# The last roots of an attention block as logarithm and exponential, and an output slab that starts on the finished tiles

## The chip, the cores and the metric

The kernel runs on one core of a Trainium2 chip. The metric is device time in microseconds (us) of one execution; shown is the median of the runs of a kernel. The engines are TensorE (PE, with its weight loads PEld), VectorE (DVE), ScalarE (ACT), GpSimd (POOL) and the DMA queue of SyncE (SP). Each engine works through its own instructions in order and waits on semaphores for the others.

## The reference, cut to what matters

One block of a model with three mixers side by side (a linear recurrent unit "LRU", an attention with forget gates "fox", and a recurrent mixer "rwkv"), whose outputs are joined and multiplied by one output matrix; a mixture of experts and two more layers follow.

```python
def rms_norm(x, g, eps=1e-6):
    return x * lax.rsqrt(jnp.mean(x * x, axis=-1, keepdims=True) + eps) * g

ya = rms_norm(gelu(gate_in) * h, lru_norm_g)                # 256 wide
o  = softmax(mask(q k^T * scale + c_i - c_j)) v             # 8 heads of 64, 512 tokens
yb = rms_norm(o, fox_norm_g)                                # 512 wide
yc = ((o_r - mean) * lax.rsqrt(var + 64e-5) * ln_g + ln_b + bonus) * g   # 256 wide
y  = concatenate([ya, yb, yc], axis=-1)
x  = x + y @ w_out
x  = x + hier_moe(rms_norm(x, norm2_g), ...)
```

## The kernel before, in words

Tokens (512) lie along the free dimension, features in tiles of 128 partitions, so a 1024-wide activation is eight tiles of 128x512. Matmul inputs are split in two parts: a tile is cast to fp32r (`y_hi`), the rest is kept (`y_lo = y - y_hi`), and three products (hi·hi, lo·hi, hi·lo) are summed. Weights come as slabs of 128x2048: SP loads `raw`, ACT casts `w_hi` (L218), POOL subtracts `w_lo` (L227).

The change lies in two blocks of code and in the step between them. The first block ends with the attention's loop over 32 units (`UNITS`: eight heads for the query block of tokens 384 to 511, then for 256 to 383, 128 to 255 and 0 to 127, so keys shrink from 512 to 128). No scheduler orders it: each engine has its own loop over n, and what stands at `if n == 24` is the order. In turn n:

- PE computes the scores of unit n into one of two banks (L1115, L1117), turns the probabilities of unit n-2 (L1127) and weighs the values of unit n-3 (L1137). The scores of n wait until the exponential of n-2 has read their bank; the weighing waits for ACT's copy of the turned probabilities.
- DVE takes the row maximum of unit n (L1739), later the inverse of the row sum (L1750), and from unit 16 on scales the weighed output into the token-major tile `o_tok` (L1729).
- ACT takes the exponential of unit n (L1427) and copies the turned probabilities of n-2 (L1401); up to unit 15 it scales the outputs (L1408). After the last head of a query block it squares that block with a sum (L1412).

The rest of the three mixers is spread over the turns. LRU's and rwkv's row sums are copied out (L1774, n = 17), their roots taken by ACT with those of the first two attention blocks at n = 21 (L1417, L1458, L1459), inverted by DVE at n = 22 (L1717, L1778), spread by PE over the partitions with matmuls against the identity (LRU at n = 24, L1088; rwkv at 25 and 26, L1098) and multiplied in by DVE (LRU L1784 at n = 24; rwkv L1705 and L1706 at 25 and 26). The first two attention blocks are turned at 27 and 28 (L1144) and written to `Y` at 28 and 29 (L1723). After the loop blocks three and four follow together: ACT loads the table of the square root (L1435), squares the last block, takes two roots; DVE inverts and scales; PE turns eight pieces (L1144); DVE writes `Y`.

Then the stage closes: an end of block on every engine, semaphores cleared, a barrier of all engines. The second block begins with ACT casting the eight tiles of `Y` to `y_hi` (L1941), DVE subtracting (L1946), and PE working through the first output slab tile by tile (L277 to L279, each tile 6 matmuls), each tile waiting for its `y_lo`. Three more slabs follow without a pause on PE; DVE adds each to `xT` (L1959), which SP loads anew at the start of this block.

A function of ACT needs its table in the engine; the built program holds an ACT_TABLE_LOAD wherever the next function is not in the table that is loaded.

Of the kernel before, what the change touches and what calls it, by code (L numbers as in the profile page):

```python
# [22 lines left out]
F32 = mybir.dt.float32  # L23
# [6 lines left out]
P = 128  # L30
# [117 lines left out]
def build(nc, t):  # L148
    with ExitStack() as whole:
# [486 lines left out]
        o_tok, o_sq = [M[:, n] for n in (0, 1, 8, 9)], T[:, 2]  # L636
# [81 lines left out]
        sums_out, lru_spread, ln_spread = (stage_sem(n) for n in ("sums_out", "lru_spread", "ln_spread"))  # L718
        gate_row = [stage_sem(f"gate_row{n}") for n in range(4)]
# [78 lines left out]
        def _(pe):  # L798
# [285 lines left out]
            def spread_lru():  # L1084
                pe.wait_ge(sums_out, 2)
# [61 lines left out]
            for n in range(len(UNITS) + 3):  # L1147
# [26 lines left out]
                if n in (27, 28):  # L1174
                    pe.wait_ge(y_rwkv, n - 26)
                    turn_block(n - 27, (seq_wu, seq_so)[n - 27])
            pe.wait_ge(y_fox, 2)
            pe.wait_ge(sc_exp, len(UNITS))
            for i in range(2, TB):
                turn_block(i, pd[i - 2])  # L1180

        @block.scalar
        def _(act):
# [231 lines left out]
            def block_roots(i, count):  # L1415
                act.wait_ge(fox_sq, i + count)
                act.activation(small[:, 48 + i:48 + i + count], small[:, 44 + i:44 + i + count], ACT.Sqrt, bias=EPS,  # L1417
                               scale=1.0 / 512).then_inc(fox_root, 1)

            for n in range(len(UNITS) + 4):  # L1420
# [13 lines left out]
                if n == len(UNITS) + 1:  # L1434
                    act.preload_act_table(ACT.Sqrt)  # L1435
# [15 lines left out]
                if n in (12, 14):  # L1451
                    j = (n - 12) // 2
                    act.wait_ge(lru_val, j + 1)
                    act.activation(lru_sqr[:, j], lh[:, j], ACT.Square).then_inc(lru_sq, 1)
                if n == 21:
                    block_roots(0, 2)
                    act.wait_ge(sums_out, 1)
                    act.activation(small[:, 64:68], small[:, 64:68], ACT.Sqrt, bias=EPS, scale=1.0 / 256)  # L1458
                    act.activation(small[:, 68:84], small[:, 68:84], ACT.Sqrt, bias=GN_EPS,  # L1459
                                   scale=1.0 / CH).then_inc(ln_root, 1)  # L1460
                if n == 26:
                    act.wait_ge(y_lru, 2)
                    split_next(act, IN1_PAIRS - 1, 1)
            block_roots(2, 2)

        @block.vector
        def _(dve):
# [264 lines left out]
            for n in range(len(UNITS) + 4):  # L1732
# [53 lines left out]
                if n in (25, 26):  # L1786
                    rwkv_out(n - 25)
                if n in (28, 29):
                    block_out(n - 28, (seq_wu, seq_so)[n - 28])
            block_inverses(2, 2)  # L1790
            for i in range(2, TB):
                scale_block(i)
            for i in range(2, TB):
                block_out(i, pd[i - 2])
# [6 lines left out]
        y_hi = sb("y_hi", [P, KT, TOK], F32R)  # L1801
        y_lo = sb("y_lo", [P, KT, TOK], F32R)
        V, QK, MG = (sb(n, [P, KT, TOK]) for n in ("V", "QK", "MG"))
# [52 lines left out]

        stage2_loaded = sem("stage2_loaded")
# [66 lines left out]
        def y_vector(dve, v, m, j, value, n, yb, vb, tj=None, wait=None):  # L1924
# [12 lines left out]
            dve.wait_ge(y_ready, yb + 2 * n + 2)  # L1937

# [153 lines left out]
        def _(pe):  # L2092
# [351 lines left out]
        def _(act):  # L2444
            a = steps["scalar"].again(act)
            round_scalar(act, Y, 0)
# [14 lines left out]
            for n in range(4):  # L2461
# [898 lines left out]
```

## Time and profile before

| | us |
|---|---|
| median of 3 runs | 2642.66 (2641.64 to 2643.73) |
| the profiled execution, its own time | 2649.67 |
| its span, first to last instruction | 2647.9 |
| PE busy | 2592.0 (98%) |
| ACT busy | 1109.7 (42%) |
| DVE busy | 1545.8 (58%) |
| mean granted clock of PE | 0.987 |

A row of the timeline gives the start in us, how long the group was busy, the engine, the line of the kernel, the operation, output<-inputs, shapes, how many instructions were merged, and in square brackets how long the engine stood idle before it and whose work released it. "Granted clock" is a share of full speed: 1.00 is 2.4 GHz, 0.50 is 1.2 GHz.

### The profile page before, as it was taken

Reading aid. Unit: us, or ns where it says so; the run is one execution under the profiler, and the core shown is the slowest. Engines: PE = TensorE matmul, PEld = TensorE weight load, DVE = VectorE, ACT = ScalarE, POOL = GpSimd, SP = SyncE. Lnnn points to the kernel's source line nnn. Section 1 sums busy time; section 2 is a strip of 40 time slices with the busy share of each in tenths; the row PEclk is TensorE's granted clock in tenths of the full one; section 3 lists DMA queues with packets and bytes.
Section 4 is the critical chain, followed back from the end, with each engine's and each line's share of the span. In section 5 each row is a group of like instructions: output and inputs, shape, how many; then the busy total and the mean of one; then the engine's idle time right before and its main releaser. Section 6 shows DMA issues by size and latency. Waiting matters only on the chain.

```text
span 2647.9 us, 32566 instructions
## 1 busy us (share of the span) xinstructions
PE 2592.0 (98%) x12974; PEld 2138.6 (81%) x12974; DVE 1545.8 (58%) x1718; ACT 1109.7 (42%) x1309; POOL 876.4 (33%) x203
## 2 busy tenths in 40 slices
PE   7999889999999999999999999999999999999998
PEld 5777778888788888888888888888888888888887
DVE  5584545999775383364674346855563463835445
ACT  5353535778534532334332223435432343422222
POOL 0211020000142443445444443432443454444444
PEclk9999888999999999999999999999999999999999
DMA  4240024999231472223233333322752232333332
GB/s 154 104 152 1 1 102 185 368 371 371 84 112 64 165 289 87 95 103 112 104 119 120 119 120 118 108 83 81 265 192 92 99 119 92 108 135 119 119 119 103
DMA packets 61292, 361.13 MB, mean 136 GB/s; under 512 B 7280, under 2 KB 8176, under 8 KB 26096
## 3 DMA queue, kind: packets, MB, share of 16 engines
q1 hardware_dynamic: 58720, 353.49, 37.4%
q10 hardware_dynamic: 2448, 5.90, 0.6%
q8 instruction: 88, 1.44, 0.2%
q14 instruction: 36, 0.29, 0.0%
HBM read 357.25 MB, written 2.10 MB: 136 GB/s over the span
## 4 chain that ended last, share of the span: by engine, by line
PE 81%; DVE 3%; ACT 1%; issue 1%; POOL 1%; DMA 0%; ACTq 0%; DVEq 0%; SPq 0%; POOLq 0%
PE pd L277 20%; PE pd L279 19%; PE pd L278 19%; PE pd L301 2%; PE pd L303 2%; PE pd L302 2%; PE pd L2215 2%; PE pd L2213 2%; PE pd L2214 2%; DVE sb_y_lo L1935 1%; PE pd L2240 1%; PE pd L2242 1%; PE pd L2241 1%; PE pd L2170 1%; PE px L2371 1%
## 5 line engine op out<-in xcount | busy, mean ns | idle before, releaser
L227 POOL TENSOR_TENSOR sb_w_lo<-sb_raw,sb_w_hi 128x2048 fp32r<-128x2048 f32 x175 | 820.3, 4687 | 1612.6 <-ACT sb_w_hi L218 1612.6
L277 PE MATMUL pd<-sb_h_hi,sb_w_hi 128*128 128x512 f32 x1600 | 631.6, 395 | 3.0 <-DVE sb_h_lo L579 2.4
L278 PE MATMUL pd<-sb_h_lo,sb_w_hi 128*128 128x512 f32 x1600 | 623.8, 390 | 0.0
L279 PE MATMUL pd<-sb_h_hi,sb_w_lo 128*128 128x512 f32 x1600 | 623.7, 390 | 0.0
L218 ACT CAST sb_w_hi<-sb_raw 128x2048 fp32r<-128x2048 f32 x181 | 346.2, 1913 | 412.8 <-PE pd L279 320.4
L277 PE MATMUL pd<-sb_y_hi,sb_w_hi 128*128 128x512 f32 x960 | 376.5, 392 | 5.1 <-DVE sb_y_lo L1946 3.9
L279 PE MATMUL pd<-sb_y_hi,sb_w_lo 128*128 128x512 f32 x960 | 374.7, 390 | 0.0
L278 PE MATMUL pd<-sb_y_lo,sb_w_hi 128*128 128x512 f32 x960 | 374.5, 390 | 0.0
L277 PEld LDWEIGHTS pd<-sb_h_hi,sb_w_hi 128*128 128x128 f32 x1600 | 301.0, 188 | 68.4 <-issue 5.3
L279 PEld LDWEIGHTS pd<-sb_h_hi,sb_w_lo 128*128 128x128 f32 x1600 | 300.9, 188 | 63.2
L278 PEld LDWEIGHTS pd<-sb_h_lo,sb_w_hi 128*128 128x128 f32 x1600 | 301.1, 188 | 61.4 <-issue 0.5
L277 PEld LDWEIGHTS pd<-sb_y_hi,sb_w_hi 128*128 128x128 f32 x960 | 180.9, 188 | 46.3 <-issue 4.8
L279 PEld LDWEIGHTS pd<-sb_y_hi,sb_w_lo 128*128 128x128 f32 x960 | 180.8, 188 | 38.1
L278 PEld LDWEIGHTS pd<-sb_y_lo,sb_w_hi 128*128 128x128 f32 x960 | 180.9, 188 | 37.3
L1935 DVE TENSOR_TENSOR sb_y_lo<-sb_T,sb_y_hi 128x512 fp32r<-128x512 f32 x80 | 187.9, 2388 | 35.8 <-ACT sb_y_hi L1909 28.6
L1961 DVE SCALAR_TENSOR_TENSOR sb_xT<-pd,sb_lay,sb_xT 128x512 f32<-128x512 f32 x80 | 56.8, 747 | 155.7 <-PE pd L279 152.0
L1904 ACT ACTIVATE sb_T<-pd 128x512 f32<-128x512 f32 x60 | 32.6, 596 | 203.8 <-PE pd L279 203.8
L593 DVE CUSTOM_DVE_ANT_0 sb_QK<-sb_QK,sb_Y 128x1024 f32<-128x1024 f32 x32 | 79.1, 2508 | 65.8 <-ACT sb_Y L2649 44.9
L301 PE MATMUL pd<-sb_w_hi,sb_h_hi 128*128 128x512 f32 x288 | 112.6, 391 | 0.0
L303 PE MATMUL pd<-sb_w_lo,sb_h_hi 128*128 128x512 f32 x288 | 112.1, 389 | 0.0
L302 PE MATMUL pd<-sb_w_hi,sb_h_lo 128*128 128x512 f32 x288 | 112.1, 389 | 0.0
L3166 DVE TENSOR_TENSOR sb_T<-sb_T 128x512 f32<-128x512 f32 x64 | 45.0, 744 | 105.5 <-ACT sb_T L1904 103.5
(581 smaller groups left out, 3755.6 us busy)
## 6 DMA issues: line engine op xcount, KB each, us to landing
sb_raw<-in_slabs SPq DMA_DIRECT2D x190, 1024.0 KB, 4.8
sb_moe_raw<-in_moe SPq DMA_DIRECT2D x56, 1024.0 KB, 5.5
sb_raw<-in_moe SPq DMA_DIRECT2D x28, 1024.0 KB, 5.4
sb_QK<-in_ada SPq DMA_DIRECT2D x32, 512.0 KB, 5.7
sb_V<-in_ada SPq DMA_DIRECT2D x32, 512.0 KB, 5.6
sb_M<-in_ada SPq DMA_DIRECT2D x16, 512.0 KB, 4.0
sb_Y<-in_ada SPq DMA_DIRECT2D x16, 512.0 KB, 5.8
sb_MG<-in_ada SPq DMA_DIRECT2D x16, 512.0 KB, 5.9
```

The source lines that it names most:

```text
L218: act.copy(w_hi[j][:], raw[j][:]).then_inc(w_hi_ready[j], 1)
L227: pool.tensor_tensor(w_lo[j][:], raw[j][:], w_hi[j][:].bitcast(F32), ALU.subtract).then_inc(w_lo_ready[j], 1)
L277: pe.matmul(out, w_hi[j][:, cols], hi[:, k], start=(k == 0), stop=False)
L278: pe.matmul(out, w_hi[j][:, cols], lo[:, k], start=False, stop=False)
L279: last = pe.matmul(out, w_lo[j][:, cols], hi[:, k], start=False, stop=(k == KT - 1))
L301: pe.matmul(pd[b][:], hi[:, k, toks], w_hi[j][:, cols], start=(k == 0), stop=False)
L302: pe.matmul(pd[b][:], lo[:, k, toks], w_hi[j][:, cols], start=False, stop=False)
L303: last = pe.matmul(pd[b][:], hi[:, k, toks], w_lo[j][:, cols], start=False, stop=(k == KT - 1))
L593: dve.tensor_tensor_reduce(tiles[slot], tiles[slot], row, 1.0, 0.0, ALU.mult, ALU.add, into).then_inc(ada_used, 1)
L1935: dve.tensor_tensor(y_lo[:, bass.ds(2 * n + f, 1)], T[:, tj + f:tj + f + 1], y_hi[:, bass.ds(2 * n + f, 1)].bitcast(F32), ALU.subtract).th ...
L1961: ins = dve.scalar_tensor_tensor(to, bank, lay[:, bass.ds(gate + tile + 2 * j + f, 1)], to, ALU.mult, ALU.add)
L2213: pe.matmul(pd[x % 2][:], hi[:, k], moe_w_hi[s][:, cols], start=(k == 0), stop=False)
```

## The change

Three things change. (1) Every root of the attention's tail becomes `exp(-0.5 * ln(x))` on ACT, which drops DVE's inversions. LRU's and rwkv's logarithms stand at n = 18 and their exponential at 19, those of the first two attention blocks at 20 and 21, that of the third at 28 and 29. (2) Spreads and outputs move: LRU's spread from 24 to 20, rwkv's from 25 and 26 to 21 and 24, the turns of attention blocks from 27, 28 and after the loop to 26, 28 and 32, the weight cast from 26 to 24, DVE's parts accordingly. (3) `y_hi` and `y_lo` are laid over the first stage's memory, so ACT can cast LRU's and rwkv's four tiles inside the loop (26, 27, 30, 31) and DVE subtract two of them (29, 32). The fourth attention block is no longer finished in the first stage: the second block's ACT squares it and takes logarithm and exponential, DVE scales, PE turns it, while PE already multiplies LRU's two tiles; then come rwkv's two tiles and last the four attention tiles.

```diff
-                if n == 24:
+                if n == 20:
                     spread_lru()
-                if n in (25, 26):
-                    spread_ln(n - 25)
+                if n in (21, 24):
+                    spread_ln((21, 24).index(n))
...
-                act.activation(small[:, 48 + i:48 + i + count], small[:, 44 + i:44 + i + count], ACT.Sqrt, bias=EPS,
-                               scale=1.0 / 512).then_inc(fox_root, 1)
+                act.activation(small[:, 48 + i:48 + i + count], small[:, 44 + i:44 + i + count], ACT.Ln, bias=EPS,
+                               scale=1.0 / 512).then_inc(fox_log, 1)
...
+                if n == 18:
+                    act.wait_ge(sums_out, 1)
+                    act.activation(small[:, 64:68], small[:, 64:68], ACT.Ln, bias=EPS, scale=1.0 / 256)
+                    act.activation(small[:, 68:84], small[:, 68:84], ACT.Ln, bias=GN_EPS,
+                                   scale=1.0 / CH).then_inc(sums_log, 1)
+                if n == 19:
+                    act.wait_ge(sums_log, 1)
+                    act.activation(small[:, 64:84], small[:, 64:84], ACT.Exp, scale=-0.5).then_inc(ln_root, 1)
+                if n == 20:
+                    block_logs(0, 2)
                 if n == 21:
-                    block_roots(0, 2)
...
+                    block_inverses(0, 2, 1)
-                if n == 26:
+                if n == 24:
                     act.wait_ge(y_lru, 2)
                     split_next(act, IN1_PAIRS - 1, 1)
-            block_roots(2, 2)
+                if n == 28:
+                    block_logs(2, 1)
+                if n == 29:
+                    block_inverses(2, 1, 2)
+                if n in (26, 27, 30, 31):
+                    k = {26: 0, 27: 1, 30: 6, 31: 7}[n]
...
+                    act.copy(y_hi[:, k], Y[:, k]).then_inc(y_hi_ready, 1)
...
+                    for i, k in enumerate(Y_ORDER):
+                        if i == 2:
+                            pe.wait_ge(last_scaled, 1)
+                            for f in range(4):
+                                last = pe.transpose(px[0][:, blocks[f]], o_last[:, blocks[f]], ident[:])
+                            last.then_inc(last_turned, 1)
+                        pe.wait_ge(y_ready, i + 1)
...
-            round_scalar(act, Y, 0)
+            act.activation(T[:, 2], o_last, ACT.Square, accum_out=last_sum).then_inc(last_sq, 1)
+            act.wait_ge(last_sq, 1)
+            act.activation(last_log, last_sum, ACT.Ln, bias=EPS, scale=1.0 / 512).then_inc(last_logged, 1)
+            act.wait_ge(last_logged, 1)
+            act.activation(last_inv, last_log, ACT.Exp, scale=-0.5).then_inc(last_root, 1)
+            split_next(act, IN1_PAIRS, 0)
+            act.wait_ge(last_out, 1)
+            for n in range(4, KT):
+                act.copy(y_hi[:, Y_ORDER[n]], Y[:, Y_ORDER[n]]).then_inc(y_hi_ready, 1)
```

How the instructions stand on ACT around the roots of the middle units before (sb_H are the exponentials, sb_small the sums and roots, sb_M<-px or pd the copies of turned probabilities):

```order
L1427 ACTIVATE sb_H,sb_small<-pd,sb_small 128x256
L1401 COPY sb_M<-pd 128x256
L1417 ACT_TABLE_LOAD
L1417 ACTIVATE sb_small<-sb_small 128x2
L1458 ACTIVATE sb_small<-sb_small 128x4
L1459 ACTIVATE sb_small<-sb_small 128x16
L1427 ACT_TABLE_LOAD
L1427 ACTIVATE sb_H,sb_small<-pd,sb_small 128x256
```

and the same place now (L1437 is the exponential of a unit, L1406 the copy; L1466 and L1467 are LRU's and rwkv's logarithms, L1471 their exponential, L1422 and L1427 those of the attention blocks):

```order
L1466 ACT_TABLE_LOAD
L1466 ACTIVATE sb_small<-sb_small 128x4
L1467 ACTIVATE sb_small<-sb_small 128x16
L1437 ACT_TABLE_LOAD
...
L1471 ACTIVATE sb_small<-sb_small 128x20
L1437 ACTIVATE sb_H,sb_small<-pd,sb_small 128x256
L1406 COPY sb_M<-px 128x256
L1422 ACT_TABLE_LOAD
L1422 ACTIVATE sb_small<-sb_small 128x2
L1437 ACT_TABLE_LOAD
L1437 ACTIVATE sb_H,sb_small<-pd,sb_small 128x256
```

One pair of table loads has become two, two units apart; a third such pair stands at units 28 and 29 (L1422, then L1437), and a fourth at the head of the second block.

On PE the step from the first to the second block before (sb_ident,sb_M are the turns of attention blocks):

```order
L1137 MATMUL pd<-sb_xT,sb_M 128x64
L1144 MATMUL pd<-sb_ident,sb_M 128x128 x8
L1797 UNCONDITIONAL_BRANCH
L2091 UNCONDITIONAL_BRANCH
L277 MATMUL pd<-sb_y_hi,sb_w_hi 128x512
L278 MATMUL pd<-sb_y_lo,sb_w_hi 128x512
L279 MATMUL pd<-sb_y_hi,sb_w_lo 128x512
```

and now, where the turn of the last block (sb_o_last) stands behind twelve matmuls of the slab:

```order
L1141 MATMUL pd<-sb_xT,sb_M 128x64
L1821 UNCONDITIONAL_BRANCH
L2127 UNCONDITIONAL_BRANCH
L2168 MATMUL pd<-sb_y_hi,sb_w_hi 128x512
L2169 MATMUL pd<-sb_y_lo,sb_w_hi 128x512
L2170 MATMUL pd<-sb_y_hi,sb_w_lo 128x512
...
L2163 MATMUL px<-sb_ident,sb_o_last 128x128 x4
L2168 MATMUL pd<-sb_y_hi,sb_w_hi 128x512
```

The eight turns have left the end of the first block: four went into the loop's turn 32, four into the slab.

## Rows read from the trace of the kernel before

**Rows 1.** Page, part 1: busy time, share of span, instructions.
```profile
PE 2592.0 (98%) x12974; PEld 2138.6 (81%) x12974; DVE 1545.8 (58%) x1718; ACT 1109.7 (42%) x1309; POOL 876.4 (33%) x203
```

**Rows 2.** Windows: length, busy PE, PEld, DVE, ACT, POOL; clock, DMA share, GB/s.
```profile
303.50:341.30 37.80, 33.18 (x218) 30.02 (x217) 19.14 (x62) 19.82 (x66) 4.53 (x1) 0.82 0.00 1
341.30:349.40 8.10, 1.94 (x8) 1.59 (x9) 3.35 (x8) 2.86 (x7) 0.00 (x0) 0.50 0.12 16
349.40:362.90 13.50, 13.49 (x48) 10.94 (x49) 4.08 (x7) 4.58 (x7) 4.61 (x1) 0.80 0.79 304
314.00:341.30 27.30, 22.68 (x174) 20.07 (x173) 17.20 (x55) 17.20 (x57) 4.53 (x1) 0.94 0.00 1
```

**Rows 3.** Timeline of ACT, units 19 to 28 of the attention loop.
```profile
315.67 0.47 ACT L1427 ACTIVATE sb_H<-pd,sb_small 128x256 f32<-128x256 f32 x1 [0.94 <-DVE sb_small L1739]
...
318.75 0.47 ACT L1427 ACTIVATE sb_H<-pd,sb_small 128x256 f32<-128x256 f32 x1 [0.57 <-DVE sb_small L1739]
...
319.22 0.36 ACT L1401 COPY sb_M<-pd 128x256 f32<-128x256 f32 x1
319.60 1.28 ACT L1417 ACT_TABLE_LOAD   x1
...
322.61 0.47 ACT L1427 ACTIVATE sb_H<-pd,sb_small 128x256 f32<-128x256 f32 x1
...
329.84 0.37 ACT L1427 ACTIVATE sb_H<-pd,sb_small 128x128 f32<-128x128 f32 x1 [3.74 <-DVE sb_small L1739]
...
335.44 0.38 ACT L1427 ACTIVATE sb_H<-pd,sb_small 128x128 f32<-128x128 f32 x1
```

**Rows 4.** Timeline of PE behind the pair of table loads.
```profile
323.49 0.66 PE L1137 MATMUL px<-sb_xT,sb_M 128*128 128x64 f32 x4 [2.27 <-ACT sb_M L1401]
```

**Rows 5.** Windows before and after that wait, columns as above.
```profile
321.20:324.20 3.00, 0.73 (x7) 0.71 (x7) 2.29 (x7) 2.94 (x8) 0.00 (x0) 1.00 0.00 0
324.20:327.60 3.40, 3.40 (x18) 3.40 (x18) 0.65 (x3) 0.72 (x3) 0.00 (x0) 0.50 0.02 5
```

**Rows 6.** Timeline of DVE, LRU's and rwkv's outputs in units 24 and 25.
```profile
327.94 1.53 DVE L1784 SCALAR_TENSOR_TENSOR sb_Y<-sb_W,sb_vec,px 128x512 f32<-128x512 f32 x2 [2.21 <-PE px L1088]
...
330.23 0.69 DVE L1705 TENSOR_TENSOR sb_M<-sb_M,px 128x512 f32<-128x512 f32 x1
```

**Rows 7.** Timeline of all engines from the last units to the second block.
```profile
340.47 1.28 ACT L1435 ACT_TABLE_LOAD   x1
...
341.02 0.28 DVE L1729 TENSOR_SCALAR sb_M<-pd,sb_small 128x64 f32<-128x64 f32 x1 [0.38 <-PE pd L1137]
341.77 0.63 ACT L1412 ACTIVATE sb_T<-sb_M 128x512 f32<-128x512 f32 x1
...
342.52 0.20 ACT L1417 ACTIVATE sb_small<-sb_small 128x2 f32<-128x2 f32 x1
...
342.96 1.01 DVE L1713 TENSOR_SCALAR sb_M<-sb_M,sb_small 128x512 f32<-128x512 f32 x2
...
343.59 1.94 PE L1144 MATMUL pd<-sb_ident,sb_M 128*128 128x128 f32 x8 [2.61 <-DVE sb_M L1713]
...
345.64 0.69 DVE L1723 TENSOR_TENSOR sb_Y<-pd,sb_vec 128x512 f32<-128x512 f32 x1 [0.16 <-PE pd L1144]
...
347.92 2.18 ACT L1941 CAST sb_y_hi<-sb_Y 128x512 fp32r<-128x512 f32 x4 [5.20 <-PEq L1800]
...
349.41 0.76 PE L277 MATMUL pd<-sb_y_hi,sb_w_hi 128*128 128x512 f32 x1 [3.88 <-DVE sb_y_lo L1946]
```

**Rows 8.** Timeline of PE: the slab's thirteenth matmul.
```profile
354.67 0.50 PE L277 MATMUL pd<-sb_y_hi,sb_w_hi 128*128 128x512 f32 x1
```

**Rows 9.** Timeline of DVE: the first slab added.
```profile
363.28 1.29 DVE L1959 TENSOR_TENSOR sb_xT<-pd,sb_xT 128x512 f32<-128x512 f32 x2 [9.80 <-PE pd L279]
```

**Rows 10.** Timeline of ACT, an exponential (L1326) and a logarithm (L1327) earlier.
```profile
133.69 0.20 ACT L1326 ACTIVATE sb_small<-sb_small 128x2 f32<-128x2 f32 x1
133.91 1.28 ACT L1327 ACT_TABLE_LOAD   x1
```

More of the change, by code:

```diff
@@ L635, in build @@
         v_att, k_att = xT[:, 0:4], xT[:, 4:8]
-        o_tok, o_sq = [M[:, n] for n in (0, 1, 8, 9)], T[:, 2]
+        y_hi, y_lo, o_last = (over(name, M, n * TOK, [P, count, TOK], dt) for name, n, count, dt in (
+            ("y_hi", 16, KT, F32R), ("y_lo", 24, KT, F32R), ("o_last", 9, 1, F32)))
+        o_last = o_last[:, 0]
+        o_tok, o_sq = [M[:, n] for n in (0, 1, 8)] + [o_last], T[:, 2]
         qk_square, qk_rstd = Y[:, 2:4], Y[:, 6:8]
@@ L1785, in _ @@
                                                    ALU.mult), y_lru, j + 1)
[L1786 to L1794, printed above, removed]
+                if n in (23, 26):
+                    rwkv_out((23, 26).index(n))
+                if n in (24, 25):
+                    scale_block(n - 24)
+                if n in (28, 30):
+                    i = (n - 28) // 2
+                    block_out(i, (seq_wu, seq_so)[i])
+                if n == 31:
+                    scale_block(2)
+                if n == 34:
+                    block_out(2, seq_wu)
+                if n in (29, 32):
+                    k = (29, 32).index(n)
+                    dve.wait_ge(y_hi_ready, k + 1)
+                    dve.tensor_tensor(y_lo[:, k], Y[:, k], y_hi[:, k].bitcast(F32),
+                                      ALU.subtract).then_inc(y_ready, 1)
+            dve.wait_ge(o_late, len(UNITS) - LATE)
         mixers.close()
@@ L1800, in build @@
         nc.all_engine_barrier()
[L1801 to L1803 removed]
+        V, QK, y_home, MG = (sb(n, [P, tiles, TOK]) for n, tiles in (("V", KT), ("QK", KT), ("y_home", 2 * KT), ("MG", KT)))
+        assert nc.lookup_mloc(y_home).addr == nc.lookup_mloc(y_hi).addr
         O = Y
@@ L1937, in y_vector, with round_rest @@
             dve.wait_ge(y_ready, yb + 2 * n + 2)
+        Y_ORDER = (0, 1, 6, 7, 2, 3, 4, 5)
+        last_sum, last_log, last_inv = (T[:, 0, n:n + 1] for n in range(3))
+        LAST_TOKENS = UNITS[-1][1]
+        def round_rest(dve, n):
+            dve.wait_ge(y_hi_ready, n + 1)
+            dve.tensor_tensor(y_lo[:, Y_ORDER[n]], Y[:, Y_ORDER[n]], y_hi[:, Y_ORDER[n]].bitcast(F32),
+                              ALU.subtract).then_inc(y_ready, 1)
         def round_scalar(act, src, yb):
@@ L2121, in _ @@
                 if n == 0:
-                    slab_rows(pe, m, j, y_hi, y_lo, (y_ready, 0))
+                    slab_starts(pe, m, 0)
+                    for i, k in enumerate(Y_ORDER):
[5 more added lines that the diff above has]
+                        pe.wait_ge(y_ready, i + 1)
+                        for f in range(2):
+                            cols = slice(k * SLAB_COLS + f * P, k * SLAB_COLS + f * P + P)
+                            pe.matmul(pd[f][:], w_hi[0][:, cols], y_hi[:, k], start=(i == 0), stop=False)
+                            pe.matmul(pd[f][:], w_hi[0][:, cols], y_lo[:, k], start=False, stop=False)
+                            last = pe.matmul(pd[f][:], w_lo[0][:, cols], y_hi[:, k], start=False, stop=(i == KT - 1))
+                    last.then_inc(slab_done[0], 1)
                     continue
@@ L2459, in keep_turned @@
                     "p (b n) -> p b n", b=TB)).then_inc(norm_hi, 1)
-            for n in range(4):
+            for n in range(1, 4):
                 if n < 3:
@@ L2770, in _ @@
             v = steps["vector"].again(dve)
-            round_vector(dve, Y, 0)
+            round_rest(dve, 2)
+            round_rest(dve, 3)
+            dve.wait_ge(last_root, 1)
+            dve.tensor_scalar(o_last, o_last, last_inv, None, ALU.mult).then_inc(last_scaled, 1)
+            dve.wait_ge(last_turned, 1)
+            gain = vec[:, V1["fox_norm"]].unsqueeze(2).to_broadcast([P, 4, P])
+            dve.tensor_tensor(Y[:, 2:6, LAST_TOKENS * P:(LAST_TOKENS + 1) * P],
+                              px[0][:].rearrange("p (k n) -> p k n", k=4), gain, ALU.mult).then_inc(last_out, 1)
+            for n in range(4, KT):
+                round_rest(dve, n)
+            dve.wait_ge(y_ready, KT)
             def turned_rest(k):
```

46 lines of the change are left out of this document (21 added, 25 removed).

## The prediction

> **What bounds the kernel now.** I read the page first: PE is busy for 98% of the span [rows 1], so a change pays only where PE stands still or runs at the lower clock. Then windows around the changed code [rows 2]: the second half of the attention loop takes 37.8 us with PE at a mean clock of 0.82, the step between the blocks takes 8.1 us of which PE works 1.94, and the first output slab takes 13.5 us without a gap. From the slab on PE never pauses for three more slabs, so whatever moves the slab's end moves the whole kernel, one to one. Two numbers decide: when the last attention output is there, 341.30 (341.02 + 0.28) [rows 7], and how long after it the first slab ends, 363.28 - 341.30 = 22.0 [rows 7, 9], of which 0.3 to 0.4 lies between PE's end (362.9, the window's end) and DVE's start. I use 21.6.
>
> In the loop three engines pass one unit along: scores on PE, maximum on DVE, exponential and copy on ACT, weighing on PE. The timelines show how little slack this has. ACT stands idle 0.94 and 0.57 us before the exponentials of units 19 and 21 [rows 3], and the one pair of table loads there (from 319.60 to the exponential at 322.61, 3.0 us with its three roots) leaves PE waiting 2.27 us [rows 4]. Behind that wait PE's clock is 0.50, that is 1.2 GHz, for 3.4 us [rows 5].
>
> **The tail, which gets shorter.** What goes from between the last output and the slab: the square root's table and the square (340.47 to 342.52), inversion, two scalings (1.01), eight turns (1.94 at 1.2 GHz), two outputs ending at 345.64 + 0.69 = 346.33, and the wait for the first cast and its remainder (347.92 to 349.41) [rows 7]. What stays is the change of stage, 347.92 - 346.33 = 1.6 us. So PE starts 1.6 us after the last output instead of 8.1. It then has twelve matmuls ready, which at the lower clock take 354.67 - 349.41 = 5.3 us [rows 7, 8], four turns (half of 1.94, 1.0), and 36 matmuls, which took 363.28 - 354.67 = 8.6 with the 0.35 behind them, so 8.25 [rows 8, 9]. Sum 1.6 + 5.3 + 1.0 + 8.25 = 16.15 against 21.6: **-5.5 us**.
>
> That takes the last block's root as hidden behind the twelve matmuls. It is a chain of its own on ACT and DVE: square 0.75 (341.77 to 342.52), load 1.28, logarithm 0.2, load 1.28, exponential 0.2, scaling 0.5 [rows 7], with hops some 4.4 us, against PE's 5.3. It fits with 0.9 to spare. If the clock were already high, PE would wait, but the slab would then end 1 to 2 us earlier all the same; if it stays low through rwkv's twelve matmuls, 12 x 0.21 = 2.5 more. Behind the turns comes DVE's output 0.69, ACT's cast (2.18 / 4 = 0.55) and DVE's remainder of about 0.65, together 2.0 with hops, against 2.7 of PE on rwkv's tiles: hidden as well, with 0.7 to spare. The second slab's weights are cast before that and need POOL's 4.61 [rows 2], over well before PE gets there. Bounds of the tail: -7 to -3.
>
> **The loop, which gets longer.** I price it in three stretches, by the exponential that opens each.
>
> *Units 19 to 21.* Before, the exponential of 21 starts at 318.75 [rows 3]. Now ACT, free at 315.67 - 0.94 = 314.73, loads the logarithm's table, takes two logarithms and loads the exponential's again: 2.9 by the pair at 319.60, so unit 19 starts at 317.6. From there ACT has no pause: exponential 0.47, copy 0.38, output 0.33, square 0.75, the exponential over 20 sums 0.2, exponential 0.47, copy 0.38, second pair 2.8 [rows 3, 7], 5.8 and some 0.3 of hops, so unit 21 starts at 323.7: **+5.0**. LRU's spread (now at 20) waits for that small exponential, but lies beside the second pair. Bounds: two pairs less the idle time they replace, 5.7 - 0.94 - 0.57 = +4.2; with PE at 1.2 GHz +6.5.
>
> *Units 21 to 28.* Before 335.44 - 318.75 = 16.7 [rows 3]. What goes: the old pair delayed unit 22 to 322.61, where a pace of 1.4 per unit would put it at 320.15, so -2.4; and unit 25 at 329.84 had waited 3.74 for a maximum [rows 3] that stood behind LRU's output on DVE (1.53, itself waiting 2.21 for PE's spread) [rows 6]. A pace of 1.2 would put it at 326.6, so -3.2. What comes: LRU's output still occupies DVE for 1.53 at unit 22, +1.1; rwkv's first spread now stands ahead of the scores of unit 22, in units where PE has no slack, +1.2; two scalings of 0.5 and two casts of 0.55, about half of them exposed, +1.2. The weight cast and rwkv's outputs (two steps of 0.69 each) [rows 6] only change units. Sum **-2.1**. Bounds: at 2.4 GHz throughout -4; at 1.2 GHz +3.
>
> *Unit 28 to the last output.* Before 341.30 - 335.44 = 5.9. The third pair costs 2.8 less about 0.8 of idle, +2.0; two casts on ACT at 30 and 31, +0.8; and DVE's scaling (0.5), remainder and output (0.69) ahead of its last two outputs, +1.0. Sum **+3.8**, bounds +2 to +5.
>
> The loop grows by 5.0 - 2.1 + 3.8 = 6.7 us. With the tail, 6.7 - 5.5 = **+1.2 us**. The profiled execution took 2649.67, 7.0 more than the median; the step moves both alike, so its like would take 2650.9 and the median goes from 2642.66 to 2643.9. What measurement can tell from no change is about 0.2%, 5.3 us, so I expect no difference.
>
> *A rule weighed.* The copy ends at 319.22 + 0.36 = 319.58, the load starts at 319.60 and takes 1.28 [rows 3]. The Trainium skill (ScalarE: Activation LUTs, "What ACT_TABLE_LOAD costs") gives 1283 ns for the load and about 1380 ns of drain besides, 2.66 us for each switch. The load agrees; before this load the trace shows no drain. By the page's figure the three pairs in the loop, less the old one, would cost 4 x 1.38 = 5.5 us more and the kernel would come out some 6 us slower, as an estimate; I go by the row.
>
> **The rivals.** *The loads fall into idle time, and the tail's gain stays.* For it: idle time of ACT before units 19, 21 and 25 [rows 3], ACT is busy only 17.2 of 27.3 us in this stretch [rows 2], and the work moved to PE's turns 20 and 21 stands just where PE waits anyway. Against it: that idle time is part of one chain through three engines, and the old pair was not absorbed [rows 4]. Taking the lower bound in the middle stretch and near the lower bounds elsewhere, 4.2 - 4 + 2 = +2, less 5.5 to 7: -3.5 to -5, some **2638.3**.
>
> *The clock falls and stays down: slower.* The place is units 20 to 31. PE's rows show 1.2 GHz behind one wait of 2.27 us [rows 4, 5]; now there are three such waits, and between them PE has less to do per unit than it has time. PE had 22.7 us of work from 314 on at a mean clock of 0.94 [rows 2]; if the last 13 us of it run at half speed they take 13 more, and as PE's steps alternate with those of DVE and ACT about half of it stands in the chain: +6. That makes 1.2 + 6 = +7.2, **2649.9**. It decides against the kernel as soon as some 8 us of PE's work run at 1.2 GHz. Against it: behind the old wait the clock came back within one stretch of 3.4 us.
>
> *One table for both functions.* In the trace an exponential (133.69) is followed by a load of 1.28 before the next logarithm [rows 10], so the two stand in different tables here, and the changed program holds a load at each change. With one table, the first stretch would keep one load (+1), the last none of its two (+1.5), the middle stay at -2.1: +0.4, and the second block's chain shrinks within its cover; 0.4 - 5.5 = -5.1, **2637.6**. The Trainium skill states that rule (ScalarE: Activation LUTs, "Table sets: the hidden batching unit"): logarithm and exponential share a set, so one load serves both. The trace of this kernel differs.
>
> **How the numbers follow.** Forecast (+1.2, of its own range -3 to +5) 0.62; hidden loads 0.17; low clock 0.18; one table 0.03. Half of the second case and most of the fourth lie beyond -5.3: faster 0.12. The low clock lies beyond +5.3 in nearly all its cases: slower 0.18. The rest, 0.70, is the same. The range for 8 in 10 runs from 2638.5 (most of the hidden case left out) to 2650 (most of the low clock taken in).
>
> **What would show it.** In the changed profile: six table loads between units 18 and 29, each pair with a wait of about 2 us on PE behind it; the exponential of unit 21 some 5 us later than 318.75, the last output near 348; PE's first slab matmul 1.6 us after it, and the slab's end 16 us after it. Wrong would be: a last output before 344 (loads hidden) or after 352 (clock), or a PE that waits in the slab for the last block's turn.

## The result and the profile after

| | before | changed |
|---|---|---|
| median of 12 runs each, us | 2643.19 | 2647.51 |
| ratio, 95% interval | | 1.0017, 1.0010 to 1.0025 |
| the profiled execution, own time / span | 2649.67 / 2647.9 | 2649.60 / 2647.8 |
| mean granted clock of PE | 0.987 | 0.989 |

The changed kernel is 0.17% slower, 4.3 us by the medians. That lies inside the predicted range and inside "no difference" by the bound of 0.2%, but above the forecast of 2643.9, and the interval leaves no change out. One of the twelve runs of the kernel before took 6987.33 us; it stands in the median above and not in the ratio. The two profiled executions are equally long, so their totals say nothing here; the stretches do. The page's first part beside [rows 1] shows 10 more instructions on ACT (the loads and split roots) and as much work on PE as before:

```profile
PE 2588.6 (98%) x12974; PEld 2134.3 (81%) x12974; DVE 1551.4 (59%) x1715; ACT 1117.2 (42%) x1319; POOL 876.4 (33%) x203
```

I cut the changed part at five marks: the exponentials of units 18, 21 and 28, the end of the last attention output (X), and DVE's first slab addition. The marks of before are 313.69, 318.75, 335.44, 341.30 and 363.28 [rows 3, 7, 9], that of unit 18 from this row of the same timeline as [rows 3]; those of the changed kernel are 310.88, 320.32, 337.63, 347.79 and 367.70.

```profile
313.69 0.47 ACT L1427 ACTIVATE sb_H<-pd,sb_small 128x256 f32<-128x256 f32 x1 [2.05 <-DVE sb_small L1739]
```

Of the changed kernel's marks the first two and the last stand in rows below; the third and the fourth (347.51 + 0.28) are these, of ACT and DVE:

```profile
337.63 0.38 ACT L1437 ACTIVATE sb_H<-pd,sb_small 128x128 f32<-128x128 f32 x1
...
347.51 0.28 DVE L1751 TENSOR_SCALAR sb_o_last<-pd,sb_small 128x64 f32<-128x64 f32 x1
```

Stretches in us:

| kernel | 18 to 21 | 21 to 28 | 28 to X | X to addition | 18 to addition |
|---|---|---|---|---|---|
| before | 5.06 | 16.69 | 5.86 | 21.98 | 49.59 |
| changed | 9.44 | 17.31 | 10.16 | 19.91 | 56.82 |
| difference | +4.4 | +0.6 | +4.3 | -2.1 | +7.2 |
| predicted | +5.0 | -2.1 | +3.8 | -5.5 | +1.2 |

The first and the third came as priced. The second and the last came 2.7 and 3.4 us worse, and the next views show why.

Ahead of unit 18 both programs do the same, yet the profiled execution of before arrived there 2.8 us later. Two window rows, of before and then of the changed kernel (columns as in [rows 2]), show PE full in both, at 1.2 GHz up to 313.95 in the one and back at 2.4 GHz from 307 on in the other:

```profile
303.70:313.95 10.25, 10.25 (x44) 9.71 (x44) 1.95 (x7) 2.56 (x9) 0.00 (x0) 0.50 0.00 0
```
```profile
307.00:310.88 3.88, 3.88 (x31) 3.59 (x30) 1.20 (x5) 1.16 (x5) 0.00 (x0) 0.99 0.00 0
```

So the difference at the addition itself is 367.70 - 363.28 = +4.4, beside +4.3 in the medians and +7.2 from unit 18. Behind the addition the execution of before lost that lead again: it took 2284.6 us to its end, the changed one 2280.1, at a clock of 0.87 against 0.91 from 366 to 460. That is why the two totals agree. What rests on one stretch of one execution is therefore tested below on other kernels.

**The slab.** Windows of the changed kernel (columns as in [rows 2]): the loop's second half, the change of stage, the slab.

```profile
303.50:347.80 44.30, 34.13 (x222) 30.14 (x222) 24.43 (x64) 26.73 (x77) 4.52 (x1) 0.81 0.00 1
347.80:349.60 1.80, 0.02 (x1) 0.05 (x1) 0.17 (x1) 0.19 (x1) 0.00 (x0) 0.50 0.00 0
349.60:367.30 17.70, 15.69 (x52) 12.19 (x53) 7.39 (x8) 7.48 (x11) 4.57 (x1) 0.76 0.73 262
```

The step between the blocks is 1.8 us instead of 8.1 [rows 2], as forecast. But the slab, which PE filled from end to end before (13.49 of 13.50), now has a hole of 2.0 us. PE's timeline in the slab names it:

```profile
349.58 0.77 PE L2168 MATMUL pd<-sb_y_hi,sb_w_hi 128*128 128x512 f32 x1 [2.29 <-PEq L1824]
...
354.84 0.61 PE L2163 MATMUL px<-sb_ident,sb_o_last 128*128 128x128 f32 x4
...
360.21 0.50 PE L2168 MATMUL pd<-sb_y_hi,sb_w_hi 128*128 128x512 f32 x1 [2.01 <-DVE sb_y_lo L1972]
```

The last block's turns (354.84) wait for nothing: its root is hidden, as the prediction had it. PE waits at 360.21 for DVE's remainder `y_lo` (L1972) of an attention tile. DVE's timeline, the form of L1972 with the min, median and max in ns of one instruction, and POOL's timeline, in that order:

```profile
356.87 5.09 DVE L1972 TENSOR_TENSOR sb_y_lo<-sb_Y,sb_y_hi 128x512 fp32r<-128x512 f32 x4 [0.69 <-ACT sb_y_hi L2503]
...
367.70 0.69 DVE L1995 TENSOR_TENSOR sb_xT<-pd,sb_xT 128x512 f32<-128x512 f32 x1 [5.74 <-PE pd L2170]
```
```profile
L1972 DVE TENSOR_TENSOR sb_y_lo<-sb_Y,sb_y_hi x6: 679/682/3285, 349.4 to 361.3; 128x512 fp32r<-128x512 f32 x6
```
```profile
330.56 4.52 POOL L227 TENSOR_TENSOR sb_w_lo<-sb_raw,sb_w_hi 128x2048 fp32r<-128x2048 f32 x1 [93.25 <-ACT sb_w_hi L218]
...
355.03 4.57 POOL L227 TENSOR_TENSOR sb_w_lo<-sb_raw,sb_w_hi 128x2048 fp32r<-128x2048 f32 x1 [19.94 <-ACT sb_w_hi L218]
```

One of the six remainders took 3.285 us instead of 0.68. The four from 356.87 take 5.09 together; the long one began while POOL's weight remainder ran (355.03 to 359.60) and ended at 356.87 + 3.285 = 360.15, just behind it. Before, ACT cast the second slab's weights behind the eight `y` casts and POOL began at 354.06, when the `y_lo` were through (353.48). After the change ACT casts the weights ahead of the attention tiles (at 353.07), and POOL runs beside those tiles' `y_lo`. Some 1.5 us after PE's wait the clock falls to 0.50 for 3.4 us (window row):

```profile
361.70:365.10 3.40, 3.40 (x9) 2.64 (x8) 0.26 (x1) 0.00 (x0) 0.00 (x0) 0.50 0.98 378
```

**The loop.** DVE's timeline in units 24 to 26, rwkv's second output, beside the 0.69 of [rows 6]:

```profile
331.01 0.69 DVE L1728 TENSOR_TENSOR sb_M<-sb_M,px 128x512 f32<-128x512 f32 x1
331.73 3.91 DVE L1729 TENSOR_TENSOR sb_Y<-sb_M 128x512 f32<-128x512 f32 x1
```

Both began while POOL's remainder of 330.56 to 335.08 ran. L1728, with one input in PSUM, took its usual 0.69. L1729, with both inputs in SBUF, took 3.91, 3.2 more. ACT's timeline shows what followed, and the loads:

```profile
310.88 0.47 ACT L1437 ACTIVATE sb_H<-pd,sb_small 128x256 f32<-128x256 f32 x1 [0.50 <-DVE sb_small L1761]
...
311.94 1.28 ACT L1466 ACT_TABLE_LOAD   x1
...
313.57 1.28 ACT L1437 ACT_TABLE_LOAD   x1
...
317.50 1.28 ACT L1422 ACT_TABLE_LOAD   x1
...
319.01 1.28 ACT L1437 ACT_TABLE_LOAD   x1
320.32 0.47 ACT L1437 ACTIVATE sb_H<-pd,sb_small 128x256 f32<-128x256 f32 x1
...
336.00 0.37 ACT L1437 ACTIVATE sb_H<-pd,sb_small 128x128 f32<-128x128 f32 x1 [3.92 <-DVE sb_small L1761]
```

The exponential at 336.00 waits 3.92 for a maximum that stands behind L1729 on DVE. It replaces the wait of 3.74 at 329.84 [rows 3] that the change removed. PE's timeline shows the waits behind the first pair of loads, behind that collision and behind the third pair (338.27):

```profile
316.05 0.63 PE L1141 MATMUL pd<-sb_xT,sb_M 128*128 128x64 f32 x4 [2.42 <-ACT sb_M L1413]
...
336.66 0.43 PE L1141 MATMUL pd<-sb_xT,sb_M 128*128 128x64 f32 x2 [3.14 <-ACT sb_M L1406]
...
341.75 0.69 PE L1141 MATMUL pd<-sb_xT,sb_M 128*128 128x64 f32 x2 [1.58 <-ACT sb_M L1406]
```

The theory for the experiments: a DVE instruction with two SBUF inputs stands still while POOL runs its weight remainder. This happens once in the loop and once in the slab, and the two together are the 6 us by which the forecast missed in the stretches. The kernel before shows the same elsewhere. This line of its page is a remainder of the same shape in later layers, with a mean of 2388 ns:

```profile
L1935 DVE TENSOR_TENSOR sb_y_lo<-sb_T,sb_y_hi 128x512 fp32r<-128x512 f32 x80 | 187.9, 2388 | 35.8 <-ACT sb_y_hi L1909 28.6
```

Its mean mixes two kinds. Of the 80, 34 began while POOL ran a weight remainder; they took 4.68 to 4.88 us, and each ended 0.55 us behind POOL. The other 46 took 0.68 to 0.69.

The rival theories: the loop's excess is its table loads and casts, and the slab's wait comes from the order of ACT's casts or from the low clock.

### The profile page after: what moved, and what is told of

It is laid out like the page before. It is cut to its first block, busy times and chain, and to the rows that moved or that the text cites. A ratio compares the mean times of both kernels' runs of the same rounds, so it can differ in the third digit from the quotient of the medians.

```text
span 2647.8 us, 32574 instructions
## 1 busy us (share of the span) xinstructions
PE 2588.6 (98%) x12974; PEld 2134.3 (81%) x12974; DVE 1551.4 (59%) x1715; ACT 1117.2 (42%) x1319; POOL 876.4 (33%) x203
## 4 chain that ended last, share of the span: by engine, by line
PE 81%; DVE 3%; ACT 1%; issue 1%; POOL 1%; DMA 0%; ACTq 0%; DVEq 0%; SPq 0%; POOLq 0%
PE pd L277 19%; PE pd L279 19%; PE pd L278 19%; PE pd L301 2%; PE pd L303 2%; PE pd L302 2%; PE pd L2262 2%; PE pd L2264 2%; PE pd L2263 2%; DVE sb_y_lo L1961 1%; PE pd L2289 1%; PE pd L2291 1%; PE pd L2290 1%; PE pd L2219 1%; PE px L2420 1%
## 5 line engine op out<-in xcount | busy, mean ns | idle before, releaser
L277 PE MATMUL pd<-sb_y_hi,sb_w_hi 128*128 128x512 f32 x944 | 369.1, 391 | 1.2 <-DVE sb_y_lo L1961 0.8
L279 PE MATMUL pd<-sb_y_hi,sb_w_lo 128*128 128x512 f32 x944 | 367.4, 389 | 0.0
L278 PE MATMUL pd<-sb_y_lo,sb_w_hi 128*128 128x512 f32 x944 | 367.4, 389 | 0.0
L1961 DVE TENSOR_TENSOR sb_y_lo<-sb_T,sb_y_hi 128x512 fp32r<-128x512 f32 x80 | 188.0, 2388 | 35.8 <-ACT sb_y_hi L1935 28.6
```

The costliest lines, as they stand in the source:

```text
L277: pe.matmul(out, w_hi[j][:, cols], hi[:, k], start=(k == 0), stop=False)
L278: pe.matmul(out, w_hi[j][:, cols], lo[:, k], start=False, stop=False)
L279: last = pe.matmul(out, w_lo[j][:, cols], hi[:, k], start=False, stop=(k == KT - 1))
L1961: dve.tensor_tensor(y_lo[:, bass.ds(2 * n + f, 1)], T[:, tj + f:tj + f + 1], y_hi[:, bass.ds(2 * n + f, 1)].bitcast(F32), ALU.subtract).th ...
```

## The experiments

Each ratio is to the kernel before, run beside it on the same chip.

| kernel | ratio, 95% interval | 18 to 21 | 21 to 28 | 28 to X | X to addition | 18 to addition |
|---|---|---|---|---|---|---|
| 1 second slab's remainder on DVE | 1.0004 (0.9995, 1.0013) | 9.75 | 16.99 | 10.16 | 15.80 | 52.70 |
| 2 rwkv's output moved | 1.0012 (1.0003, 1.0021) | 9.75 | 14.09 | 9.47 | 19.95 | 53.26 |
| 3 no loads in the loop | 1.0004 (0.9994, 1.0013) | 6.08 | 16.79 | 7.53 | 19.95 | 50.35 |
| 4 before, cast early | 1.0021 (1.0012, 1.0030) | 4.62 | 20.60 | 6.47 | 20.98 | 52.67 |
| 5 edits 1 and 2 | 0.9994 (0.9985, 1.0003) | 9.82 | 14.01 | 9.46 | 15.88 | 49.17 |
| 6 one pair in the loop | 0.9977 (0.9967, 0.9986) | 7.30 | 14.78 | 6.15 | 15.56 | 43.79 |

**1. The second slab's weight remainder moves from POOL to DVE, behind the `y_lo`.**

```diff
 # second block, POOL
-            remainder(pool, IN1_PAIRS, 1)
 # second block, DVE
             dve.wait_ge(y_ready, KT)
+            remainder(dve, IN1_PAIRS, 1)
```

> In the changed kernel the third of the last four remainders of y on DVE... more exactly the first of them takes 3.28 us instead of 0.68, while POOL subtracts the weight remainder of the second output slab (355.03 to 359.60); PE waits 2.01 us for it and then runs 3.4 us at 1.2 GHz. Here that weight remainder is done by DVE after its y remainders, so POOL does nothing then. Theory 'DVE stands while POOL works': the 3.28 falls to 0.7, PE has no wait inside the slab, the slab ends 16.2 us after the last attention output instead of 19.9, the time falls by 3.5 to about 2644.0. Rival 'DMA and ACT traffic' (xT is loaded and ACT casts at the same time): the remainder stays at about 3 us, and the time rises by up to 1, as DVE now has 2.3 us more to do.

DVE's timeline of this kernel in the slab:

```profile
356.25 2.50 DVE L1972 TENSOR_TENSOR sb_y_lo<-sb_Y,sb_y_hi 128x512 fp32r<-128x512 f32 x4 [0.69 <-ACT sb_y_hi L2502]
...
358.79 2.29 DVE L227 TENSOR_TENSOR sb_w_lo<-sb_raw,sb_w_hi 128x2048 fp32r<-128x2048 f32 x1
...
363.14 1.29 DVE L1995 TENSOR_TENSOR sb_xT<-pd,sb_xT 128x512 f32<-128x512 f32 x2 [2.06 <-PE pd L2169]
```

The four remainders take 2.50 instead of 5.09, and PE works 13.77 of 13.80 us in the slab (window row):

```profile
349.10:362.90 13.80, 13.77 (x53) 11.26 (x54) 7.14 (x9) 7.52 (x11) 0.00 (x0) 0.82 0.68 239
```

From X to the addition it is 15.80, 4.1 less than with POOL: 2.0 of PE's wait, and the rest fits the 3.4 us at half clock behind it, which would cost 1.7 (an estimate from the window row of the changed kernel). The loop stays as it was. So the collision, not the order of the casts (which is kept), makes the slab's wait. The remainder itself costs less on DVE, 2.29 against 4.57. The median is 2645.27, 1.3 above the expected 2644.0.

**2. The loop's weight cast one unit later, rwkv's second output one earlier, both scalings in turn 24.**

```diff
-                if n in (23, 26):
-                    rwkv_out((23, 26).index(n))
-                if n in (24, 25):
-                    scale_block(n - 24)
+                if n in (23, 25):
+                    rwkv_out((23, 25).index(n))
+                if n == 24:
+                    scale_block(0)
+                    scale_block(1)
 # ACT
-                if n == 24:
+                if n == 25:
                     act.wait_ge(y_lru, 2)
```

> In the loop of the changed kernel the second step of rwkv's second output on DVE (two tiles in SBUF) takes 3.91 us instead of 0.69 while POOL subtracts the weight remainder of the first slab (330.56 to 335.08). Here rwkv's second output stands one unit earlier (25), both scalings of attention blocks at 24, and the weight cast one unit later (25), so that POOL starts after it. Theory 'DVE stands while POOL works': that step takes 0.7, ACT's wait of 3.92 before the exponential of unit 27 shrinks to under 1, the last output comes 2.5 to 3 us earlier, the time is about 2644.5. Rival 'table loads and clock alone make the loop longer': the step may shorten but the last output moves by less than 1, time 2647.0 to 2648.0.

DVE's timeline of this kernel, and then POOL's:

```profile
330.14 0.69 DVE L1729 TENSOR_TENSOR sb_Y<-sb_M 128x512 f32<-128x512 f32 x1
...
335.45 1.33 DVE L1817 TENSOR_TENSOR sb_y_lo<-sb_Y,sb_y_hi 128x512 fp32r<-128x512 f32 x1 [0.18 <-DVE sb_small L1772]
```
```profile
331.70 4.53 POOL L227 TENSOR_TENSOR sb_w_lo<-sb_raw,sb_w_hi 128x2048 fp32r<-128x2048 f32 x1 [94.96 <-ACT sb_w_hi L218]
```

L1729 is through before POOL begins and takes 0.69 again. Units 21 to 28 take 14.09 instead of 17.31, 3.2 less, which is the 3.2 that L1729 had lost. The next DVE instruction with two SBUF inputs, a `y_lo`, now meets POOL's last 0.8 us and is 0.64 longer. The slab, which this edit leaves alone, keeps its 19.95. From unit 18 the last output comes 3.6 us earlier, where 2.5 to 3 were expected; the median of 2645.66 is 1.2 above the expected one.

**3. The three logarithms in the loop become copies.** ACT's `Identity` stands for `Ln`, so no table changes there; the roots of LRU, rwkv and the first three attention blocks are not computed.

```diff
-                    act.activation(small[:, 64:68], small[:, 64:68], ACT.Ln, bias=EPS, scale=1.0 / 256)
+                    act.activation(small[:, 64:68], small[:, 64:68], ACT.Identity, bias=EPS, scale=1.0 / 256)
 # and likewise the sums 68:84 and block_logs
```

> The changed kernel with the logarithms in the loop (units 18, 20, 28) replaced by the identity, which every table has, so its six table loads in the loop are gone; the roots there are left uncomputed. All else stands, the collision of DVE and POOL too. Theory 'the pairs stand in the chain': each pair costs 2 us or a little more, exponential of unit 21 is 4 to 5 us earlier relative to that of unit 18, the last output 5 to 6 us earlier, the time about 2642. Rival 'loads hide in idle time, the loop is longer by the collision alone': under 1.5 us, 2646 or more.

Rows of this kernel, ACT's timeline and then DVE's:

```profile
310.63 0.47 ACT L1437 ACTIVATE sb_H<-pd,sb_small 128x256 f32<-128x256 f32 x1 [0.50 <-DVE sb_small L1761]
...
316.71 0.47 ACT L1437 ACTIVATE sb_H<-pd,sb_small 128x256 f32<-128x256 f32 x1 [1.60 <-DVE sb_small L1761]
...
331.87 0.37 ACT L1437 ACTIVATE sb_H<-pd,sb_small 128x128 f32<-128x128 f32 x1 [3.92 <-DVE sb_small L1761]
```
```profile
327.61 3.90 DVE L1729 TENSOR_TENSOR sb_Y<-sb_M 128x512 f32<-128x512 f32 x1
```

From unit 18 to X it takes 30.40 instead of 36.91, where 5 to 6 less were expected: three pairs cost 6.5 us, 2.2 each on the mean, where a pair lasts about 2.8 on ACT. The loads are exposed, not hidden. L1729 still takes 3.90 and ACT still waits 3.92, so the collision is independent of the loads. By the ratio the gain over the changed kernel is smaller than by the stretch, 0.13% or 3.4 us, with about as much uncertainty, and the median of 2644.68 stands between the 2642 expected and the rival's 2646.

**4. The kernel before, with nothing changed but the weight cast, two units earlier.**

```diff
-                if n == 26:
+                if n == 24:
                     act.wait_ge(y_lru, 2)
```

> The kernel before with one edit: ACT's weight cast of the loop at unit 24 instead of 26. Theory 'DVE stands while POOL works': POOL's subtraction of 4.5 us now begins some 2 us after LRU's output and covers the second step of one of rwkv's outputs, which then takes 3 to 4 us instead of 0.69; the last output comes 2 to 3 us later, the time is 2645 to 2646. Rival 'the cast is free to move': all steps of DVE keep their 0.69, the time stays within 1 us of the kernel before, 2642 to 2644.

Its DVE timeline, then POOL's, then ACT's:

```profile
328.19 0.69 DVE L1706 TENSOR_TENSOR sb_Y<-sb_M 128x512 f32<-128x512 f32 x1
...
331.27 2.55 DVE L1706 TENSOR_TENSOR sb_Y<-sb_M 128x512 f32<-128x512 f32 x1
```
```profile
328.23 5.04 POOL L227 TENSOR_TENSOR sb_w_lo<-sb_raw,sb_w_hi 128x2048 fp32r<-128x2048 f32 x1 [91.67 <-ACT sb_w_hi L218]
```
```profile
326.18 1.90 ACT L218 CAST sb_w_hi<-sb_raw 128x2048 fp32r<-128x2048 f32 x1 [3.52 <-DVE sb_Y L1784]
...
334.18 0.37 ACT L1427 ACTIVATE sb_H<-pd,sb_small 128x128 f32<-128x128 f32 x1 [4.32 <-DVE sb_small L1739]
```

The early cast alone makes the collision, and both orders stand in these rows. DVE's first L1706 began 0.04 us ahead of POOL, kept its 0.69, and POOL took 0.5 longer than its usual 4.53. The second began while POOL ran and took 2.55, ending at 333.82, after POOL's 333.27. Units 21 to 28 take 20.60 instead of 16.69. Not all of these 3.9 us are the collision's: here the cast, and the exponential of unit 25 behind it, first wait 3.52 for LRU's output (L1784), and unit 26, counted from unit 21, is already 1.3 us later than before; the other 2.6 come with the second L1706, at unit 27. In the changed kernel LRU's output is earlier and its cast waits for nothing. The kernel is slower by 0.21%, about as much as the whole change costs. Its median of 2650.44 lies 4 us above what was expected, and its profiled run, 2645.25, is the shortest of its eleven.

**5. Edits 1 and 2 together.**

```diff
-            remainder(pool, IN1_PAIRS, 1)
+            remainder(dve, IN1_PAIRS, 1)      # behind the y_lo
-                if n in (23, 26):
+                if n in (23, 25):                 # rwkv_out; scale_block(0), (1) at 24, weight cast at 25
```

> Both edits that took DVE out of POOL's way together: the second slab's weight remainder on DVE, and in the loop rwkv's second output at unit 25 with the weight cast at 25. If the two collisions are independent, their savings add: from the exponential of unit 18 to the first slab's addition 56.8 - 4.1 - 3.6 = 49.1 us, level with the 49.6 of the kernel before; time within 1.5 us of the kernel before in the same call. Rival 'what one edit frees the other loses' (the step waits elsewhere): 51 or more, time 2 us above the kernel before.

Without the two collisions the four stretches stand to before at +4.8, -2.7, +3.6 and -6.1, against the forecast's +5.0, -2.1, +3.8 and -5.5. From unit 18 to the addition it is 49.17, as expected, 0.4 under before. The ratio of 0.9994 can't be told from no change; the medians, 2641.56 against 2644.70, lie further apart than the 1.5 us expected. One small meeting is left, the `y_lo` of experiment 2, here 1.33 us long.

**6. Edit 1, one pair of loads in the loop, and the third attention block finished with the fourth.**

```diff
 # ACT, loop: all logarithms at n = 20, all exponentials at 21; weight cast at 25
-                if n == 18:
+                if n == 20:
                     act.wait_ge(sums_out, 1)
...
-                if n == 28:
-                    block_logs(2, 1)
-                if n == 29:
-                    block_inverses(2, 1, 2)
 # DVE, loop: both scalings at 22, LRU's output at 23, rwkv's at 24 and 25, y_lo at 32 and 33
 # second block: Ln and Exp on two sums, eight turns instead of four
-            act.activation(last_log, last_sum, ACT.Ln, bias=EPS, scale=1.0 / 512).then_inc(last_logged, 1)
+            act.activation(last_log, late_sums, ACT.Ln, bias=EPS, scale=1.0 / 512).then_inc(last_logged, 1)
```

> Besides the remainder of the second slab on DVE, only one pair of table loads in the loop instead of three: all logarithms of sums at unit 20, their exponentials at 21; LRU's spread at 22, rwkv's at 23 and 24, its outputs at 24 and 25, weight cast at 25; the third attention block's root is taken in the second block together with the fourth's, where a pair of loads stands anyway; two of the y remainders of the loop at 32 and 33. Theory (table pairs cost 2.2 us each in the loop, collisions 3.2 and 3.7): from unit 18 to the first addition 49.1 - 4.3 + 1.5 (four more turns, one more scaling and output in the second block) = 46, time 3 to 4 us below the kernel before. Rival (with the loads gone the loop is bound by PE at 1.2 GHz or by DVE, nothing is left to win): 48.5 or more, time level with the kernel before.

Windows of this kernel from 303.50 to X, the change of stage, and the slab; and below, the first table load of each of its two pairs on ACT:

```profile
303.50:338.33 34.83, 29.82 (x227) 26.28 (x225) 19.74 (x62) 21.98 (x74) 4.53 (x1) 0.95 0.01 1
338.33:340.20 1.87, 0.00 (x0) 0.00 (x0) 0.25 (x1) 0.27 (x1) 0.00 (x0) 0.94 0.00 0
340.20:353.60 13.40, 13.35 (x56) 11.02 (x57) 8.00 (x11) 7.41 (x11) 0.00 (x0) 0.88 0.69 245
```
```profile
314.39 1.28 ACT L1462 ACT_TABLE_LOAD   x1
...
340.67 1.28 ACT L2485 ACT_TABLE_LOAD   x1
```

The loop keeps a mean clock of 0.95 instead of 0.81, the slab stays full although it turns two blocks, and from unit 18 to the addition it is 43.79, 5.8 less than before, where 46 was expected. Its median is 2636.97 against 2644.70, where a gain of 3 to 4 us was expected: this version beats both kernels, by 0.23% the one before. The edits were made together, so what each is worth here isn't shown.

## Why the prediction came out as it did

**The net.** The direction came out: a loop that grows by more than the tail gives back. The size missed by 3 us, +4.3 against +1.2 in the medians, and by 6.0 in the stretches from unit 18 (+7.2), of which 3.4 lie in the tail and 2.7 in units 21 to 28. The stretch from unit 18 to the addition puts the changed kernel, five of the six experiments and the kernel before in the order of their medians, from 43.79 and 2636.97 to 56.82 and 2647.51. That is a coarse order: the kernel before had medians of 2643.19, 2644.51 and 2644.70 in its three sets of runs. Experiment 4 falls out of it (52.67 and 2650.44, with runs from 2645.3 to 2653.4). Why the medians show 3 us less than the stretches for the change as a whole stays open; the 2.8 us that before's execution lost ahead of unit 18 would do it if its other executions lose them too, but experiment 4, the same program up to unit 24, was there at 310.09. On the other side, five of the changed kernel's twelve runs took 2646.5 to 2646.7 us, 3 less than the profiled one, and no trace shows where. That the median came within 3.6 us of the forecast is therefore in part luck: by the stretch of 7.2 it would have been 2649.9.

**Tail, -5.5: the term was mis-sized, measured -2.1.** Its parts held. PE started 349.58 - 347.79 = 1.8 after the last output (1.6 said), and the root's chain was hidden behind twelve matmuls. The step that failed is the sentence that the second slab's weights "need POOL's 4.61 [rows 2], over well before PE gets there". It asked only when POOL is done, and not whom POOL holds up meanwhile. The remainder after which PE had 0.7 to spare took 3.285 instead of 0.65. With that removed the tail is -6.2 (experiment 1). The page of before had the sign, L1935 with its mean of 2388 ns.

**Units 21 to 28, -2.1: mis-sized, measured +0.6.** The failed step is that the weight cast and rwkv's outputs "only change units". The cast triggers POOL, and POOL's 4.5 us now fell over rwkv's second output: experiment 2 takes that away and measures -2.6, and experiment 4 makes the same collision in the kernel before, where it costs 2.6 of 3.9 us. In the kernel before the same work of POOL stood where DVE reads PSUM in each long instruction; its POOL timeline, and the DVE rows inside that span:

```profile
334.57 4.53 POOL L227 TENSOR_TENSOR sb_w_lo<-sb_raw,sb_w_hi 128x2048 fp32r<-128x2048 f32 x1 [97.28 <-ACT sb_w_hi L218]
```
```profile
335.29 0.69 DVE L1723 TENSOR_TENSOR sb_Y<-px,sb_vec 128x512 f32<-128x512 f32 x1
...
337.17 0.69 DVE L1723 TENSOR_TENSOR sb_Y<-px,sb_vec 128x512 f32<-128x512 f32 x1
```

Both outputs took 0.69, while rwkv's last step (L1706) had ended at 333.82, before POOL began.

**Units 18 to 21, +5.0, and 28 to X, +3.8: right, measured +4.4 and +4.3.** Without the pairs (experiment 3) the two stretches take 6.0 us less, 3.4 and 2.6. Not every pair left "about 2 us" of PE's wait, as was said: behind the second one PE was busy throughout, since LRU's spread of eight matmuls stood there (1.66 us) and its clock had fallen to 0.50 after the first pair's wait of 2.42.

**The rivals.** *Hidden loads* fell with experiment 3. *The low clock* took part, but not as the cause: units 28 to X ran at 0.51 (0.99 before), behind the wait of 3.14 that the collision made. With that wait gone (experiment 2) they ran at 0.82 and took 9.47 instead of 10.16, a share of 0.7 us; in the slab it had the 1.7 of experiment 1. That this rival had named +7.2, the figure that the stretch came to, is chance: experiment 5 keeps the loads' waits, and without the two collisions nothing of the 7.2 is left. The window rows of units 28 to X, of before and then of experiment 2:

```profile
335.44:341.30 5.86, 4.48 (x33) 3.57 (x31) 4.35 (x16) 3.75 (x17) 3.65 (x1) 0.99 0.00 1
```
```profile
334.09:343.56 9.47, 5.64 (x33) 4.59 (x31) 7.31 (x20) 6.72 (x21) 2.13 (x1) 0.82 0.01 2
```

*One table for both* fell with the rows: a load stands between every logarithm and exponential (311.94, 313.57).

## What to carry to other kernels

When an edit moves an instruction, ask what it triggers on another engine and where that now lies. An earlier weight cast moved 4.5 us of POOL's work over DVE's critical steps; the same move alone made the kernel before 0.21% slower, by that and by the cast's own wait for its data. Look for DVE instructions that read SBUF alone inside POOL's long elementwise spans, and put PSUM readers there, or let DVE do the work itself once it is past its own chain. Such a stop looks like a long instruction, not like a wait: compare a line's longest instruction with its shortest. Gather roots that change ACT's table into as few pairs as the loop allows: one pair less was worth 2.2 us here, and the pair inside the slab of experiment 6, which PE fills for 13.35 of 13.40 us, cost nothing that its rows show.

## What the runs showed of the hardware

A DVE `TENSOR_TENSOR` of 128x512 with both inputs in SBUF took 3.91, 3.90, 3.285, 2.55 and 1.33 us where it began during POOL's subtraction of 128x2048, and 0.68 to 0.69 in these stretches elsewhere; in the whole kernel before, 34 of the 80 of line L1935 met POOL and took 4.68 to 4.88. With one input in PSUM it took 0.69 within the same span of POOL (331.01). Where DVE was first, POOL was the longer by 0.5 (5.04). The Trainium skill (SBUF — State Buffer, "SBUF: two separate sides") states the rule: DVE and GpSimd share a pair of ports as an exclusive lock, whoever starts first holds it for the whole instruction, and the other blocks fully; among the DVE operations that take it are those with two SBUF inputs against a GpSimd operation that reads SBUF. The rows agree: the DVE instruction that came second ended 0.55 us behind POOL's end each time (335.64 against 335.08 in the loop, 360.15 against 359.60 in the slab, 333.82 against 333.27 in experiment 4). A DVE scaling whose one tile comes from SBUF stood still too. In the kernel before, two of the eight of this line began during POOL's subtraction, one at 952.98 beside 952.80 to 957.53, and took 5.10 us instead of 0.75:

```profile
L3089 DVE TENSOR_SCALAR sb_V<-sb_V,sb_small x8: 742/751/5100, 951.7 to 1922.4; 128x1024 f32<-128x1024 f32 x8
```

Three stops of PE cost more than their length: behind the waits of 2.42, 3.14 and 2.01 us the granted clock was 0.50 or 0.51, for 2.8, 10 and 3.4 us. The window rows of the changed kernel for the first two (the third stands above):

```profile
317.50:320.30 2.80, 2.80 (x13) 2.62 (x13) 0.42 (x1) 2.77 (x3) 0.00 (x0) 0.50 0.00 0
...
337.63:347.79 10.16, 7.68 (x33) 6.21 (x31) 6.46 (x20) 6.70 (x21) 0.00 (x0) 0.51 0.01 2
```

In the second of these rows PE works 7.68 of 10.16 us, with short waits between, and the clock stays low to its end; in the slab PE is busy without a pause behind its wait, and after 3.4 us the clock is back.
